# Feed-forward up products: x_hi and x_lo side by side under one load of the high weights

## The reference

```
def swiglu(x, w_in, w_out):
    gu = x @ w_in                                # (256, 1024) @ (1024, 2 * 2816)
    g, u = gu[..., :D_FF], gu[..., D_FF:]
    return (jax.nn.silu(g) * u) @ w_out          # (256, 2816) @ (2816, 1024)

x = layer_norm_2(ALPHA_2 * x + 0.5 * swiglu(x, ffn_w_in[l, i], ffn_w_out[l, i]), ...)
```

## Time and profile before

| | us |
|---|---|
| three runs | 1846.11, 1845.65, 1843.27; median 1845.65 |
| profiled execution | 1844.63 |
| its span, first to last instruction | 1842.90 |
| TensorE matmuls busy | 1703.1 (92%) |
| VectorE busy | 715.3 (39%) |
| ScalarE busy | 446.4 (24%) |

### The profile page before, as it was taken

One profiled execution on the slowest core, in us unless ns is written; L12 is line 12 of the kernel. 1 busy time (PEld: TensorE's weight loads), 2 busy tenths in 40 slices (PEclk: granted clock), 3 DMA queues, 4 the chain that ended last, 5 costly groups with the idle time before them and its releaser, 6 DMA issues.

```text
span 1842.9 us, 21717 instructions
## 1 busy us (share of the span) xinstructions
PE 1703.1 (92%) x9124; PEld 1190.8 (65%) x9124; DVE 715.3 (39%) x991; ACT 446.4 (24%) x511; POOL 61.6 (3%) x104
## 2 busy tenths in 40 slices
PE   8996898889888887999999599999999999999998
PEld 7744222222222225999874359998999977769997
DVE  1665311111111115544510845446544523345445
ACT  1331100000000002433200214443434303314442
POOL 2000000000000000000100000000000000000000
PEclk9997999999999998999999799999999996599999
DMA  7506499999999999655324136554655422037500
GB/s 208 204 26 249 175 395 395 394 393 394 394 394 394 394 396 365 208 182 184 113 91 157 49 132 236 192 177 158 205 196 189 160 70 90 1 132 237 192 34 23
DMA packets 220045, 395.22 MB, mean 214 GB/s; under 512 B 10914, under 2 KB 111392, under 8 KB 219984
## 3 DMA queue, kind: packets, MB, share of 16 engines
q1 hardware_dynamic: 217248, 385.67, 58.8%
q0 software_dynamic: 2736, 8.68, 1.3%
HBM read 393.28 MB, written 1.05 MB: 214 GB/s over the span
## 4 chain that ended last, share of the span: by engine, by line
PE 64%; DMA 23%; DVE 8%; SPq 3%; issue 2%; ACT 1%; POOL 1%; POOLq 0%; DVEq 0%; ACTq 0%
PE bank L1234 26%; DMA ring<-in_moe_w_dram 22%; PE bank L1247 11%; PE bank L823 3%; PE bank L1439 3%; PE bank L1365 3%; PE bank L639 2%; PE bank L1350 2%; PE bank L1655 2%; PE bank L1643 1%; SPq L255 1%; PE bank L1681 1%; PE bank L1222 1%; PE bank L586 1%; PE bank L803 1%
## 5 line engine op out<-in xcount | busy, mean ns | idle before, releaser
L823 PE MATMUL bank<-ring,arena 128*64 128x512 f32 x1024 | 267.2, 607 | 50.8 <-DMA ring<-in_moe_w_dram 46.8
L823 PEld LDWEIGHTS bank<-ring,arena 128*64 128x64 f32 x1024 | 78.1, 138 | 217.7 <-issue 120.2
L1234 PE MATMUL bank<-x_hi,split_u_hi 128*128 128x256 f32 x688 | 195.0, 283 | 0.0
L1234 PE MATMUL bank<-x_hi,split_u_lo 128*128 128x256 f32 x688 | 194.7, 283 | 0.0
L1234 PE MATMUL bank<-x_lo,split_u_hi 128*128 128x256 f32 x688 | 194.7, 283 | 0.0
L1234 PE MATMUL bank<-x_lo,split_g_hi 128*128 128x256 f32 x656 | 185.6, 283 | 0.0
L1234 PE MATMUL bank<-x_hi,split_g_lo 128*128 128x256 f32 x656 | 185.6, 283 | 0.0
L1234 PE MATMUL bank<-x_hi,split_g_hi 128*128 128x256 f32 x656 | 185.6, 283 | 0.0
L1160 DVE TENSOR_TENSOR split_g_lo<-ring,split_g_hi 128x2048 fp32r<-128x2048 f32 x47 | 107.7, 2292 | 138.0 <-ACT split_g_hi L1154 138.0
L1014 DVE SCALAR_TENSOR_TENSOR arena<-arena,work 128x256 f32<-128x256 f32 x32 | 15.4, 480 | 344.5 <-PE bank L852 344.5
L1160 DVE TENSOR_TENSOR split_u_lo<-ring,split_u_hi 128x2048 fp32r<-128x2048 f32 x45 | 103.2, 2292 | 75.7 <-ACT split_u_hi L1154 75.7
(11 more groups left out here) (319 smaller groups left out, 2360.2 us busy)
## 6 DMA issues: line engine op xcount, KB each, us to landing
ring<-in_moe_w_dram SPq DMA_DIRECT2D x192, 1024.0 KB, 13.5
ring<-in_ffn_w_in_dram SPq DMA_DIRECT2D x88, 1024.0 KB, 5.1
ring<-in_ffn_w_out_dram SPq DMA_DIRECT2D x44, 1024.0 KB, 4.9
ring<-in_ml_w_in_dram SPq DMA_DIRECT2D x12, 1024.0 KB, 5.0
ring<-in_rec_w_in_dram SPq DMA_DIRECT2D x10, 1024.0 KB, 11.7
ring<-in_at_w_in_dram SPq DMA_DIRECT2D x6, 1024.0 KB, 5.1
ring<-in_rec_w_out_dram SPq DMA_DIRECT2D x5, 1024.0 KB, 14.0
gb_row<-in_ln_g_dram POOLq DMA_DIRECT2D x8, 512.0 KB, 7.0
```

The source lines that it names most:

```text
L823: i = nc.tensor.matmul(bank[4 + p][64 * j:64 * j + 64, :], xe[p][:, k, :], unit_view(n, 4)[:, k % 4, :], start=(k == 0), stop=(k == KT - 1))
L1234: i = nc.tensor.matmul(up_bank(kind, s_)[:, m * T:(m + 1) * T], w, xp_[b][:, k, :], start=(k == 0 and j == 0), stop=(k == KT - 1 and j == 2))
```

## The change

x_hi and x_lo are interleaved: for each contraction tile k the 256 columns of x_hi lie beside the 256 of x_lo. In `up`, w_hi meets both in one matmul of 512 columns, which fills a whole bank: w_hi by x_hi in the first half, w_hi by x_lo in the second. w_lo by x_hi is added into the first half, in a matmul of 256 columns. So each half m of a product has a bank of its own (`up_bank(kind, m)`: banks 4 and 5 for g, 6 and 7 for u), and the same banks serve every step. On the way out ScalarE copies the second half to SBUF (`second_part`, into silu or h_raw), and VectorE adds the first half from the bank (`add_first_part`). Silu then works in place in SBUF, and the product of silu and u has both operands in SBUF. TensorE waits for the add of the step before (f_gsum, f_usum) before it writes a bank again. Step 0's g product stays as it was. In both engines' orders the split of the next u unit changes place against h_hi and h_lo.

```diff
-        x_hi, x_lo = [nc.alloc_sbuf_tensor_at(f"x_{part}", [P, KT, T], F32R, offset=parts_at + i * KT * T * 4)
-                      for i, part in enumerate(("hi", "lo"))]
+        x_both = nc.alloc_sbuf_tensor_at("x_both", [P, KT, 2, T], F32R, offset=parts_at)
+        x_hi, x_lo = x_both[:, :, 0, :], x_both[:, :, 1, :]
...
-        def up_bank(kind, s_):
-            return bank[kind if s_ == 0 else 4 + 2 * (s_ % 2) + kind]
+        def up_bank(kind, m):
+            return bank[4 + 2 * kind + m]
...
         def ffn_act(act, f):
+
+            def second_part(kind, to, s):
+                for m in range(2):
+                    i = nc.scalar.activation(to[:, m, :], up_bank(kind, m)[:, T:2 * T], ACT.Copy)
+                i.then_inc(s, 1)
+
             split_act(act, f, 1, 0)
             for s_ in range(NSTEP):
                 c = NSTEP * f + s_
                 act.wait_ge(f_mm[0], c + 1)
                 if c:
                     act.wait_ge(f_h, c)
-                nc.scalar.activation(silu, up_bank(0, s_)[:].rearrange("p (a t) -> p a t", a=2),
-                                     ACT.Silu).then_inc(f_silu, 1)
+                if s_ > 0:
+                    second_part(0, silu, f_gpart)
+                else:
+                    nc.scalar.activation(silu, bank[0][:].rearrange("p (a t) -> p a t", a=2), ACT.Silu).then_inc(f_silu, 1)
                 split_act(act, f, *((0, s_ + 1) if s_ < NSTEP - 1 else (2, s_)))
+                if s_ > 0:
+                    act.wait_ge(f_gsum, c - f)
+                    nc.scalar.activation(silu, silu, ACT.Silu).then_inc(f_silu, 1)
+                act.wait_ge(f_mm[1], c + 1)
+                if c:
+                    act.wait_ge(f_hhi, c)
+                    act.wait_ge(f_hlo, c)
+                second_part(1, h_raw, f_upart)
+                if s_ < NSTEP - 1:
+                    split_act(act, f, 1, s_ + 1)
                 act.wait_ge(f_h, c + 1)
                 nc.scalar.activation(h_hi[:, s_ % 2], h_raw, ACT.Copy).then_inc(f_hhi, 1)
                 if s_ < NSTEP - 1:
-                    split_act(act, f, 1, s_ + 1)
                     split_act(act, f, 2, s_)
 
         def ffn_dve(dve, f):
+
+            def add_first_part(kind, to, s):
+                for m in range(2):
+                    i = nc.vector.tensor_tensor(to[:, m, :], up_bank(kind, m)[:, 0:T], to[:, m, :], ALU.add)
+                i.then_inc(s, 1)
+
             split_dve(dve, f, 1, 0)
             for s_ in range(NSTEP):
                 c = NSTEP * f + s_
+                if s_ > 0:
+                    dve.wait_ge(f_gpart, c - f)
+                    add_first_part(0, silu, f_gsum)
                 split_dve(dve, f, *((0, s_ + 1) if s_ < NSTEP - 1 else (2, s_)))
+                dve.wait_ge(f_upart, c + 1)
+                add_first_part(1, h_raw, f_usum)
                 dve.wait_ge(f_silu, c + 1)
-                dve.wait_ge(f_mm[1], c + 1)
-                if c:
-                    dve.wait_ge(f_hhi, c)
-                    dve.wait_ge(f_hlo, c)
-
-                nc.vector.scalar_tensor_tensor(out=h_raw, in0=silu, scalar=0.5,
-                                               in1=up_bank(1, s_)[:].rearrange("p (a t) -> p a t", a=2),
+                dve.wait_ge(f_usum, c + 1)
+                nc.vector.scalar_tensor_tensor(out=h_raw, in0=silu, scalar=0.5, in1=h_raw,
                                                op0=ALU.mult, op1=ALU.mult).then_inc(f_h, 1)
+                if s_ < NSTEP - 1:
+                    split_dve(dve, f, 1, s_ + 1)
                 dve.wait_ge(f_hhi, c + 1)
                 nc.vector.tensor_tensor(h_lo[:, s_ % 2], h_raw, h_hi[:, s_ % 2].bitcast(F32), ALU.subtract).then_inc(f_hlo, 1)
                 if s_ < NSTEP - 1:
-                    split_dve(dve, f, 1, s_ + 1)
                     split_dve(dve, f, 2, s_)
...
             def up(kind, s_, c):
 
                 pe.wait_ge(f_lo[kind], c + 1)
+                if kind == 0 and s_ > 1:
+                    pe.wait_ge(f_gsum, c - f - 1)
+                if kind == 1 and s_ > 0:
+                    pe.wait_ge(f_usum, c)
+                w_hi, w_lo = place_of(f, kind, s_)
                 for m in range(2):
+                    o = up_bank(kind, m)
                     for k in range(KT):
-                        for j, (a, b) in enumerate(pairs):
-                            w = place_of(f, kind, s_)[a][:, k * FSTEP + m * P:k * FSTEP + (m + 1) * P]
-                            i = nc.tensor.matmul(up_bank(kind, s_)[:, m * T:(m + 1) * T], w, xp_[b][:, k, :],
-                                                 start=(k == 0 and j == 0), stop=(k == KT - 1 and j == 2))
+                        at = slice(k * FSTEP + m * P, k * FSTEP + (m + 1) * P)
+                        nc.tensor.matmul(o[:], w_hi[:, at], x_both[:, k].rearrange("p a t -> p (a t)"),
+                                         start=(k == 0), stop=False, skip_group_check=True)
+                        i = nc.tensor.matmul(o[:, 0:T], w_lo[:, at], x_hi[:, k, :], start=False, stop=(k == KT - 1),
+                                             skip_group_check=True)
                 i.then_inc(f_mm[kind], 1)
```

More of the change, by code:

```diff
@@ L328, in build @@
         f_mm = [sem(f"ffn_mm_{k}") for k in "gud"]
+        f_gpart, f_gsum, f_upart, f_usum = sem("ffn_gpart"), sem("ffn_gsum"), sem("ffn_upart"), sem("ffn_usum")
         f_silu, f_h, f_hhi, f_hlo = sem("ffn_silu"), sem("ffn_h"), sem("ffn_hhi"), sem("ffn_hlo")
@@ L1123, in build @@
         pairs = ((0, 0), (0, 1), (1, 0))
-        xp_ = (x_hi, x_lo)
         hp_ = (h_hi, h_lo)
@@ L1221, in up_first @@
                             for w, x in ((w_hi, x_lo),) if low else ((w_hi, x_hi), (w_lo, x_hi)):
-                                i = nc.tensor.matmul(up_bank(0, 0)[:, m * T:(m + 1) * T], w[:, at], x[:, k, :],
+                                i = nc.tensor.matmul(bank[0][:, m * T:(m + 1) * T], w[:, at], x[:, k, :],
                                                      start=(not low and m == 0 and k == 0 and w is w_hi),
```

## The result

| us | before | changed |
|---|---|---|
| median of 20 runs each | 1845.37 | 1849.21 |
| lowest to highest | 1843.27 to 1849.02 | 1847.55 to 1851.99 |
| profiled execution, span | 1842.9 | 1848.1 |
| mean granted clock of the span | 0.955 | 0.948 |
| VectorE, ScalarE busy | 715.3, 446.4 | 774.5, 494.6 |

The ratio is 1.0021, with a 95% interval of 1.0015 to 1.0027: slower, by 3.8 us, outside the range given.

What follows compares the result with a forecast made beforehand. The prediction took TensorE's stream to bound the steps; -16.0 us from the stream and +6.6 at the layer ends made -9.4, from 1844.63 to 1835.2, and 1836.3 us against the median. The 8-in-10 range was 1832 to 1846.

Steps and rivals of the forecast that it cites:

- What bounds the kernel: Feed-forward steps: only TensorE's unbroken stream counts, 16.98 us per step, with no other engine between its pieces.
- What is taken from the stream: Up products: a 512 plus a 256 replaces three 256s, saving 11.9 ns each for 1344, 16.0 us.
- What is added beside the stream: Within steps: ScalarE's copies and VectorE's adds, some 35 us more busy time each, cost nothing, with over 5 us spare.
- The tight start of layer 0: First steps of layer 0: u split ready with 0.3 us to spare; cost nothing, 1 us as upper end.
- What is added on the path: Each layer's last step: copies and adds lengthen TensorE's idle gap by 1.66 us, 6.6 us over four layers.
- The rival of the falling clock: Layer ends: longer gap lowers the clock, 3.8 us per layer; chance 0.05 for all four, 0.15 for two or three.
- The rule of the Trainium skill: Up stream: N/2.4 + 2.5 ns per matmul saves an estimated 3.4 us, so the change loses 3.2 us.
- The sum: Whole kernel: -16.0 + 6.6 = -9.4 us, with the clock at nothing; forecast time 1836.3 us.

Runs made afterwards that it cites:

- e4: Changed kernel with the 8 matmuls of 512 columns of each half m first, then the 8 of 256; 1843.47 us.
- e7: Changed kernel with up matmul sizes in runs of two (512, 512, 256, 256); 1842.35 us, one run.
- e6: Changed kernel with 10 unread identity matmuls in TensorE's gap before each layer's last down products; 1844.51 us.
- e10: e2 with 10 unread identity matmuls in TensorE's gap before each layer's last down products; 1852.36 us.
- e2: Kernel before, with only the last step's u product of each layer in the new form (4 of 84 products); 1855.02 us.
- e1: Changed kernel with only the last step's u product of each layer back to three 256-column matmuls in one bank, without copies and adds; 1839.82 us.
- e5: Changed kernel with e4's order and the last step's u product in the old form, as in e1; 1831.12 us.
- e8: Changed kernel computing w_lo by x_lo as well, so that every up matmul has 512 columns; 1980.3 us, one run.
- e11: Kernel before with x_hi and x_lo interleaved in one tensor and nothing else changed; 1846.02 us.
- e3: Changed kernel with 16 unread 128x128 identity matmuls in TensorE's gap before each layer's last down products; 1845.84 us.
- e9: Changed kernel with e7's order and the last step's u product in the old form; 1830.77 us.

## Why the prediction was wrong, by its own steps

**What bounds the kernel**: right. In every run the steps stayed one unbroken stream of TensorE.

**What is taken from the stream**: this step failed, in its size. The prediction priced the new pair by adding a 512 from a stream of 512s and a 256 from a stream of 256s: 347.8 ns, a gain of 16.0 us. Alternating, the pair takes 353 ns, and the four streams gained 8.7 us. The range of the term, zero to 17.9, held that, but no reason for a value between was thought of: a price taken from unmixed streams was carried over to a mixed one. The 11.51 us and 5.47 us pieces have only one size each, and the trace of the kernel before held a warning in the second. Its timeline of a down piece (pairs of matmuls merged), behind the 256s of an up product:

```profile
761.78 0.63 PE L1247 MATMUL bank<-split_d_hi,h_hi 128*128 128x512 f32 x2
762.25 0.62 PE L1247 MATMUL bank<-split_d_lo,h_hi 128*128 128x512 f32 x2
762.71 0.62 PE L1247 MATMUL bank<-split_d_hi,h_lo 128*128 128x512 f32 x2
763.17 0.61 PE L1247 MATMUL bank<-split_d_hi,h_hi 128*128 128x512 f32 x2
763.62 0.62 PE L1247 MATMUL bank<-split_d_lo,h_hi 128*128 128x512 f32 x2
```

Two take 0.47, 0.46 and 0.46 us before they take 0.45; singly the first five stand at 233, 236, 229, 232 and 231 ns, the rest at 227. The mean of 227.9 hides it. Ordered by size, e4 has 348.3 ns and e7 348.0, the forecast's own number.

**What is added beside the stream**: right in that it costs nothing. TensorE never waited for the added work within a step. Its size was off: ScalarE and VectorE took 48 and 59 us more busy time, not some 35 each. The prediction's own prices, 84 pairs at 0.84 and 0.76 us, make 71 and 64; the 35 does not follow from them. The tight start of layer 0 held: no idle time stands before L1263 or L1265.

**What is added on the path**: right, a little high. The copies took 0.67 us, the low bound, and not the 0.84 of the row with another function; the gap grew by 1.47 us instead of 1.66, in four layers 5.9 instead of 6.6.

**The rival of the falling clock**: this is the second step that failed. The sum has the clock at nothing; I gave two or more layers 0.20, and it happened, in two of four in this profile. Its price was too high for one fall (3.8 against the 1.6 measured), since the clock came back after 3.3 us and only part of the 18 matmuls ran low. But its place was seen too narrowly: 4.7 us came with the gap by e6 against the changed kernel, about 2.7 by e10 against e2, the start of the next layer included. The weighing against it, dense work before and behind, did not hold: eleven full steps stand before each of the gaps in the tally above, and 11 of 20 had a fall behind them. Nor was the fall of the earlier trace rows one between two dense stretches, as the prediction has it: ahead of that gap of 2.10 us TensorE had been idle for 5.21 us and then busy for 4.16 of 4.85 us at a mean granted clock of 0.55.

**The rule of the Trainium skill** (TensorE: Matmul & The Clock Gate, Back-to-back issue gap) of N/2.4 + 2.5 ns led to a loss of 3.2 us, an estimate close to the measured 3.8, but by luck: neither pitch it gives (109.2 and 215.8 ns) was seen here (119.9 and 227 in unmixed streams), and the stream gained 8.7 us where it allows an estimated 3.4.

**The sum**: -8.7 + 5.9 = -2.8 us without the clock. With the measured +3.8, some 6.6 us are the clock's or unexplained. Filling the gap returns 4.7 of it; the other 2 stay open. Neither failed step alone takes the time out of the range: with the stream's true size the forecast would have been 1843.6, and with the 6.6 us added to it alone about 1843. Falls at the start of layer 2 or 3 stand in the changed kernel, e1, e2, e4, e5, e7, e8 and e10, and not in the kernel before, e11, e3, e6 and e9, in one profile each. That e1 and e5 have them with the short gap, and e9 does not, says that the gap is not their only cause; e11 excludes the layout. Whether they come with the change or with chance stays open; nothing was tried on the norms' own gaps.

## What to carry to other kernels

Price a matmul by the pitch in its own mixture of sizes, not by the pitch in a stream of its kind: alternating 512 and 256 columns cost 5 ns a pair here, and putting runs of one size together brought it back. Work moved off TensorE was free where the stream covered it and paid in full where a layer ended: there the old, shorter form for the one last product is worth its 16 x 7 ns. And where a change lengthens an idle gap of TensorE, as from 0.84 to 2.31 us here, price what follows the gap at the lower clock as well.

## What the runs showed that I had not expected

- A change of size costs on one side and gives some back on the other: behind a run of 256s the next 512s stand at 233, 236, 228, 233 and 231 ns before 227, while the first 256s behind 512s stand at 113 and 119 ns before 120. In an unbroken alternation the sum is 353 ns, in runs of two 348.0, in runs of eight 348.3.
- Useless work helped: 10 matmuls with no reader in each of four gaps made the changed kernel 4.7 us faster, and e2 about 2.7 us faster.
- What is left to chance is as large as the change: the kernel before spans 1843.3 to 1849.0 us over 20 runs of one program, and the stretches outside the feed-forward layers, whose work never changed, differ by up to 4.7 us between profiles.
